# Latent attention: rotary parts of queries and keys stored on all 128 partitions, zeros past the 64 rows

## What is computed

```python
def mla_mixer(x, positions, w_in, q_norm_g, kv_norm_g, w_uq, w_ukv, w_out):
    c_q, c_kv, k_rope = jnp.split(x @ w_in, [MLA_Q_RANK, MLA_Q_RANK + MLA_KV_RANK], axis=-1)
    q = (rms_norm(c_q, q_norm_g) @ w_uq).reshape(B, S, MLA_HEADS, MLA_NOPE + MLA_ROPE)
    q_nope, q_rope = jnp.split(q, [MLA_NOPE], axis=-1)
    q_rope = rotary(q_rope, positions)
    ...
    s = jnp.einsum('bqhd,bkhd->bhqk', qn, k_nope) + jnp.einsum('bqhd,bkd->bhqk', qr, k_rope)
    p = jax.nn.softmax(s.astype(jnp.float32) * scale, axis=-1).astype(v.dtype)
    o = jnp.einsum('bhqk,bkhd->bqhd', p, v)
```

## Time and profile before

| | |
|---|---|
| median of 3 runs | 2674.02 us (2672.93 to 2675.98) |
| the profiled execution | 2675.73 us, span of its records 2673.8 us |
| mean granted clock of TensorE | 0.965 |
| PE busy | 2502.3 us |
| DVE busy | 2002.8 us |
| ACT busy | 1107.6 us |
| POOL busy | 295.2 us |

### The profile page before, as it was taken

How to read it: one execution, slowest core, us unless ns; L and a number is a source line. 1 busy time by engine, 2 the same in 40 slices (tenths; PEclk the granted TensorE clock), 3 DMA queues, 4 the chain that set the end, 5 groups by cost and what they waited for, 6 DMA issues and landing times.

```text
span 2673.8 us, 41581 instructions
## 1 busy us (share of the span) xinstructions
PE 2502.3 (94%) x16494; PEld 2249.2 (84%) x16494; DVE 2002.8 (75%) x3049; ACT 1107.6 (41%) x1660; POOL 295.2 (11%) x122
## 2 busy tenths in 40 slices
PE   7998999999999999698999999999999698898999
PEld 7877998999988888567998999988888587787987
DVE  6568797999867766748797999866766766555675
ACT  3341344444454554120344444445455253334333
POOL 0000595000000000000495000000000102000000
PEclk9998999999999999779999999999999899898999
DMA  6544676666677777322676666677777441144545
GB/s 219 172 134 139 195 212 192 185 189 185 201 242 260 236 241 242 117 79 95 195 212 196 180 187 187 199 247 255 243 241 242 120 140 49 63 127 125 168 149 173
DMA packets 201425, 483.65 MB, mean 181 GB/s; under 512 B 24080, under 2 KB 93712, under 8 KB 200720
## 3 DMA queue, kind: packets, MB, share of 16 engines
q1 hardware_dynamic: 197632, 472.42, 57.2%
q10 hardware_dynamic: 3600, 8.57, 0.9%
HBM read 446.30 MB, written 34.60 MB: 180 GB/s over the span
## 4 chain that ended last, share of the span: by engine, by line
PE 56%; DVE 30%; POOL 5%; DMA 4%; ACT 3%; issue 2%; ACTq 0%; DVEq 0%; SPq 0%
PE psum L1029 26%; PE psum L805 19%; DVE rounded L1475 9%; DVE halves L2410 8%; DVE halves L2407 5%; POOL rounded L778 5%; PE psum L982 4%; DMA sb<-in_u_turned 3%; PE psum L1139 1%; DVE rounded L1471 1%; ACT rounded L2828 1%; ACT rounded L2492 1%; DVE sb L1510 1%; PE psum L1107 1%; PE psum L1105 1%
## 5 line engine op out<-in xcount | busy, mean ns | idle before, releaser
L1475 DVE TENSOR_TENSOR rounded<-sb,rounded 128x1024 fp32r<-128x1024 f32 (+3 forms) x696 | 813.0, 1174 | 409.6 <-ACT rounded L2828 231.4
L2828 ACT ACTIVATE rounded<-sb 128x1024 fp32r<-128x1024 f32 x512 | 542.7, 1060 | 788.6 <-PE psum L1029 333.2
L982 PE MATMUL psum<-rounded 128*128 128x256 f32 x6144 | 775.2, 285 | 14.4 <-POOL rounded L778 14.2
L982 PEld LDWEIGHTS psum<-rounded 128*128 128x128 f32 x6144 | 748.1, 192 | 18.0 <-POOL rounded L778 18.0
L1029 PE MATMUL psum<-rounded,weights 128*128 128x512 f32 x3072 | 697.5, 389 | 1.7 <-DVE weights L2419 1.3
L1029 PEld LDWEIGHTS psum<-rounded,weights 128*128 128x128 f32 x3072 | 576.4, 188 | 122.2 <-issue 2.9
L805 PE MATMUL psum<-rounded 128*128 128x256 f32 (+1 forms) x3924 | 599.5, 315 | 43.0 <-DVE rounded L1475 34.5
L805 PEld LDWEIGHTS psum<-rounded 128*128 128x128 f32 x3924 | 548.9, 197 | 90.8 <-DVE rounded L1475 28.3
L778 POOL TENSOR_TENSOR rounded<-sb,rounded 128x1024 fp32r<-128x1024 f32 x96 | 268.8, 2815 | 1178.0 <-ACT rounded L2828 1177.5
L2492 ACT ACTIVATE rounded<-sb 128x1024 fp32r<-128x1024 f32 (+2 forms) x222 | 206.8, 943 | 326.4 <-PE psum L805 206.5
L2410 DVE TENSOR_TENSOR halves<-halves,small 128x1536 bf16<-128x1536 bf16 x128 | 225.0, 1758 | 4.4
(11 more groups left out here) (366 smaller groups left out, 1521.4 us busy)
## 6 DMA issues: line engine op xcount, KB each, us to landing
sb<-in_u_turned SPq DMA_DIRECT2D x256, 512.0 KB, 4.0
sb<-in_peer_v SPq DMA_DIRECT2D x256, 512.0 KB, 3.5
hidden<-sb SPq DMA_DIRECT2D x256, 128.0 KB, 4.0
sb<-hidden SPq DMA_DIRECT2D x256, 128.0 KB, 3.4
sb<-in_ret_w_in SPq DMA_DIRECT2D x48, 512.0 KB, 3.9
sb<-in_ffn_w_up SPq DMA_DIRECT2D x40, 512.0 KB, 4.0
sb<-in_peer_w_q SPq DMA_DIRECT2D x32, 512.0 KB, 3.9
sb<-in_ffn_w_down SPq DMA_DIRECT2D x22, 512.0 KB, 4.2
```

What stands on the lines that cost most here:

```text
L982: mm = pe.matmul(ps(bank, 1)[:, 0:T], u[p][:, k * P:(k + 1) * P], hT[:, q, k, :], start=(k == 0 and w == 0), stop=(k == KD - 1 and w == 2))
L1475: vec.tensor_tensor(ring_lo[0:k, part, 0:wide], ring[0:k, slot, 0:wide], ring_hi[0:k, part, 0:wide].bitcast(F32), ALU.subtract).then_inc(c ...
L2828: act.activation(ring_hi[:, n % SPLIT, :], ring[:, n % RING, :], ACT.Copy).then_inc(tile_hi, 1)
```

## The change

`krT` and `qrT` become tiles on all 128 partitions; their columns, and so all addresses, stay as they were. DVE and ACT write rows 0 to 63 as before. POOL zeroes rows 64 to 127 once, at the start of the phase mla, and raises a new semaphore, `rope_padded`, twice. PE waits for it ahead of the scores. L1107 then contracts over 128 partitions, as L1105 does, half of them zeros; the sums are the same.

```diff
-                a["krT"] = m.take(T, parts=ROPE)
+                a["krT"] = m.take(T)
                 a["qnT"], a["knT"] = m.take(MLA_HEADS, T), m.take(MLA_HEADS, T)
-                a["qr"], a["qrT"] = m.take(TB, MLA_HEADS, ROPE), m.take(MLA_HEADS, T, parts=ROPE)
+                a["qr"], a["qrT"] = m.take(TB, MLA_HEADS, ROPE), m.take(MLA_HEADS, T)
...
+            def pool_mla(a):
+                gp.wait_ge(phase_done, phases.index("mla"))
+                gp.memset(a["krT"][ROPE:], 0.0).then_inc(rope_padded, 1)
+                gp.memset(a["qrT"][ROPE:], 0.0).then_inc(rope_padded, 1)
+
             for phase in phases:
+                if phase == "mla":
+                    pool_mla(A[phase])
...
                 wait_all(toks[4:])
+                pe.wait_ge(rope_padded, 2)
                 for n in range(2):
...
-                vec.tensor_copy(a["krT"], ps(2, 1, ROPE)[:, T:]).then_inc(*own.next())
+                vec.tensor_copy(a["krT"][0:ROPE], ps(2, 1, ROPE)[:, T:]).then_inc(*own.next())
...
-                act.activation(a["qrT"].rearrange("p a b -> p (a b)"), ps(4, 4, ROPE), ACT.Copy).then_inc(*own.mark(act_served))
+                act.activation(a["qrT"][0:ROPE].rearrange("p a b -> p (a b)"), ps(4, 4, ROPE), ACT.Copy).then_inc(*own.mark(act_served))
```

More of the change, by code:

```diff
@@ L398, in build @@
         input_loaded, params_loaded, phase_done = sem("input_loaded"), sem("params_loaded"), sem("phase_done")
-        mem_loaded = sem("mem_loaded")
+        mem_loaded, rope_padded = sem("mem_loaded"), sem("rope_padded")
         q_taken = []
```

## The result

| | before | changed |
|---|---|---|
| median of 5 runs | 2674.02 us (2671.49 to 2678.96) | 2657.64 us (2653.40 to 2661.90) |
| profiled execution, its span | 2675.73, 2673.8 | 2657.64, 2655.8 |
| mean granted clock | 0.965 | 0.971 |

The ratio is 0.9934 with a 95% interval of 0.9916 to 0.9952: 17.6 us less (12.8 to 22.5). A repetition in 6 runs gave 0.9921 (0.9906 to 0.9935). One execution of a later variant, the one with the second pause filled, took 3500.37 us at a mean granted clock of 0.648 and is left out of its median and range.

What follows compares the result with a forecast made beforehand. The prediction took the latent attention's scores, 35.22 us on PE, slowed by height changes and a half clock, as the bound. 21.8 - 1.7 - 0.85 = 19.2 us saved gave 2655 us, range 2650 to 2662.

Steps and rivals of the forecast that it cites:

- Scores, 13.8 us at full clock: The 32 score calls, at equal height and 0.432 us each, take 13.8 us instead of 35.22, saving 21.4 us.
- The price of a change of height: In the scores, each switch between 128 and 64 partitions costs 0.19 us at full clock, 0.29 us at half.
- Why the clock was low: Alternating scores stayed at 0.50 for 33.4 us; without alternation the clock comes back or does not fall.
- Fall behind the pause ahead of the scores, even, 0.85 us: Clock fall after the 2.26 us pause before the scores; even whether it goes away, so 0.85 us is charged.
- Given back behind the scores, 1.7 us: Pause before the second L849 grows from 2.13 to 3.6 us; 3.4 us at half clock follow, costing 1.7.
- POOL at no cost: Two memsets on POOL, 2.3 us, end 48 us ahead of the first score and cost 0.
- The sum: Over the whole kernel, 21.8 - 1.7 - 0.85 = 19.2 us saved; 2654.8 from the median of the runs.
- Height does not matter: Rival, chance 0.05: score calls keep their 0.62 us whatever the height; no change, 2674.
- the clock at half through dense full-height calls: Rival, chance 0.06: denser scores stay at half clock, 0.864 us per call, 27.6 us; 7.6 us saved, 2666.5.
- That turned probabilities do not count: Rival, chance 0.1: pause and both turns are one idle stretch; second L849 and start of L1119 at half; 2657.5.
- The clock lost for good behind the scores: Rival, chance 0.04: clock drops before second L849, returns only after mla_out; 30.5 us against 21.8 won, 2682.7.

Runs made afterwards that it cites:

- second pause filled: Changed kernel plus five unused 128 x 256 products in the pause ahead of the second turn of the probabilities; median 2651.08 us, ratio 0.9902.
- fours: Kernel before, no zeros, score calls ordered four over 128 partitions, then four over 64; median 2654.89 us, ratio 0.9930.
- pairs: Kernel before, no zeros, score calls ordered two over 128 partitions, then two over 64; 2677.30 us in one execution.
- Calls of one height, over 64 partitions: Kernel before, but calls on the unrotated part contract over their first 64 channels only, the other 64 left out; 2657.98 us in one execution.
- the clock made to fall: 20 unused two-column products ahead of the scores in the changed kernel, the fours and runs of eight; 2658.66, 2659.62 and 2655.36 us.
- first pause filled: Kernel before, alternating calls kept, plus five unused 128 x 256 products in PE's pause ahead of the scores; 2659.57 us in one execution.
- runs of eight: Kernel before, no zeros, eight calls over 128 partitions then eight over 64, twice, with 20 small products ahead of the scores; 2655.36 us.

## Why the prediction was right, and where not

- *Scores, 13.8 us at full clock.* 13.89. The price of a change of height was right at both levels: 0.19 us in fours at 1.00, 0.29 in pairs at 0.50. The Trainium skill, TensorEngine Tiling (Array Packing), in "Key Properties", says that a change of tiling mode drains the engine. Lost time of 0.19 and 0.29 us at each change would fit that; no row here names the modes of these calls or shows a drain.
- *Why the clock was low.* This step failed: "the gaps between their halves are the only thing that sets them apart". Calls of one height, over 64 partitions, have no gaps and were at 0.50 for 26 us all the same; calls of one height over 128, with the clock made to fall, had it back within 3.8 us. So height by itself is enough to part a low clock from a full one, and the clock is 15.2 of the 21.3 us that the scores lost. The number came out since zeros take away the gaps and the half height at once; that is luck as far as the mechanism goes. Whether the gaps add to it in the alternating calls of the kernel before, and whether gaps at full height would keep the clock down, was not tried.
- *Fall behind the pause ahead of the scores, even, 0.85 us.* Of the four profiled executions of the changed scores with nothing put ahead of them, the clock fell in one, that with the second pause filled. Both occur, and a fall cost 1.7 us there (15.6 us for the scores instead of 13.9), as the prediction had it.
- *Given back behind the scores, 1.7 us.* The mechanism was right. In the profiled execution the term was too small: 11.49 - 8.52 = 2.97 us, from a stretch at half of 6.7 us and not 3.4. But that one is the outlier. Over the eight profiled executions with an unfilled pause of 3.27 to 3.43 us here, the turn and the products took 1.3 to 1.7 us more than 8.52 in six (1.35 in the repetition, 1.62 with the memsets made four times, 1.67 with the first pause filled before alternating calls, 1.54, 1.69 and 1.32 where the clock was made to fall), 2.97 in the changed kernel and nothing in the fours: 1.5 us in the mean, near the 1.7 charged. With the pause filled it was gone in both profiled executions.
- *POOL at no cost.* Right in sum: 2.4 us of memsets, 48 us ahead of their reader. The collision that was only bounded does happen: the splits end 0.7 us later, and the wait behind them covers it.
- *The sum.* 19.2 us from the median of three gives 2654.8; measured 2657.64, 16.4 less, and 18.0 by the spans. In the profiled execution two misses nearly cancel, which is luck: 1.3 us more was given back behind the scores, and the 0.85 for a fall ahead of them was not paid.
- *Rivals.* "Height does not matter" fell with the first trace; the clock at half through dense full-height calls did not occur, in the changed kernel or when the clock was made to fall. It is what does happen at half height. That turned probabilities do not count: its 2657.5 is the nearest number to the measured one, by chance. In the changed kernel the clock came back while PE ran L1127 behind the second turn, so that trace can't part the two. The calls of one height over 64 can: 26 us of them did not raise the clock, and it was up 0.6 us after the end of the turn that followed, with nothing else on PE. So this rival fell (and the 5.3 us for which it put the products at half have no row behind them). Such a turn does not always do it: in the pairs the clock was still at half behind one. (In the kernel before, too, the clock rose behind the turn, some 0.3 us after its end, and not during it as the prediction says.) The clock lost for good behind the scores: 6.7 us in the changed kernel, where 43.6 were needed.

## What to carry to other kernels

Where a float32 phase runs at half clock although PE is never idle, look at the number of contracted partitions: calls over 64 cost the same time as calls over 128, but they did not bring the clock back, while it rose during one run of four calls over 128. Zeros up to 128 rows, another order of the same calls, or work in the pause that drops the clock each cured it here, and the order costs nothing. Count the changes of height as well, at about 0.2 us each (0.3 at half clock); and read the price of a stretch from start times, since PE that counts as busy throughout hid 21 us here.

## What the runs showed that was not expected

- Matmuls over 64 partitions, back to back at half clock, were not given the full clock in 25.4 us; over 128 partitions, with a fall 1.1 us into the scores, it took 3.4 us.
- At full clock, alternating calls kept it (20.0 us at 1.00), and so did runs of eight over 64 partitions, 3.65 us each, between runs over 128. Whether calls over 64 alone would keep it for long was not tried. So the state at the start of a phase decided some 15 us of it.
- Pairs (two over 128, two over 64) stayed at half for 29 us and fours came back after 3.4, with the same share of either height: 14 us between two orders of the same 32 calls (30.7 and 16.7 us).
